# Moving work across the seam between two blocks of a hybrid attention and expert kernel: output weights' subtraction, context outputs, first latent exponentials

## The reference, cut to what matters

```
qkv = (x * (1 + scale) + shift) @ w_in          # 8 neighbourhood heads, 4 differential heads
context:  dense attention and differential attention over the 128 context keys
latent:   neighbourhood attention (window + context keys + relative bias), and
          differential attention over context and latent keys:  softmax(q1 k1) - lambda * softmax(q2 k2)
o = concat(na_o, rms_norm(df_o) * g * (1 - lambda_init)) @ w_out
x = layer_norm(alpha * x + gate * o);  then 16 experts, each choosing its tokens, SwiGLU;  layer_norm
```

## Time and profile before

| | us |
|---|---|
| median of 3 runs (lowest, highest) | 1845.98 (1843.43, 1846.46) |
| time of the profiled execution | 1844.35 |
| its span in the trace | 1842.5 |
| TensorE busy | 1782.4 (97%) |
| VectorE busy | 1119.4 (61%) |
| ScalarE busy | 589.7 (32%) |
| GpSimd busy | 101.4 (6%) |
| mean granted clock of TensorE | 0.985 |

### The profile page before, as it was taken

The page is one execution under the profiler, slowest core; times in us unless marked ns, Lnnn a source line. Parts: engine busy times, 40 slices in busy tenths (PEclk is TensorE's granted clock), DMA queues, the critical chain, the costliest instruction groups (busy, mean ns, idle before and its releaser), DMA issues.

```text
span 1842.5 us, 37553 instructions
## 1 busy us (share of the span) xinstructions
PE 1782.4 (97%) x15484; PEld 739.9 (40%) x15484; DVE 1119.4 (61%) x3401; ACT 589.7 (32%) x1265; POOL 101.4 (6%) x86
## 2 busy tenths in 40 slices
PE   8999989993999999999999999999999999999998
PEld 8999867762222222222222222222222222222222
DVE  3766856666647474746556474747474664747474
ACT  3222446551323232233223232322232222323233
POOL 0000132204000000000000000000000000000000
PEclk9999989996999999999999999999999999999999
DMA  9644331236999999999999999999999999999992
GB/s 381 251 166 166 121 122 60 64 147 263 375 407 406 411 422 407 424 410 425 410 425 405 425 405 416 415 409 425 404 425 410 425 405 425 408 422 410 415 415 105
DMA packets 102986, 637.13 MB, mean 346 GB/s; under 512 B 11584, under 2 KB 21824, under 8 KB 30112
## 3 DMA queue, kind: packets, MB, share of 16 engines
q1 hardware_dynamic: 97696, 618.19, 81.8%
q0 software_dynamic: 4832, 16.50, 3.2%
q10 hardware_dynamic: 288, 0.03, 0.0%
HBM read 620.02 MB, written 13.88 MB: 344 GB/s over the span
## 4 chain that ended last, share of the span: by engine, by line
PE 74%; ACT 1%; DVE 0%; issue 0%; DVEq 0%; ACTq 0%
PE ps L1630 49%; PE ps L1645 25%; ACT place L1736 0%; ACT place L1732 0%; ACT place L1739 0%; ACT place L1734 0%; DVE place L1747 0%; PE ps L1614 0%; DVE place L1807 0%; DVE place L1823 0%; PE ps L1674 0%; DVE place L1804 0%; DVEq L1573 0%; ACT place L1729 0%; ACT place L1711 0%
## 5 line engine op out<-in xcount | busy, mean ns | idle before, releaser
L1630 PE MATMUL ps<-place 128*32 128x512 f32 x4872 | 530.2, 594 | 0.8 <-DVE place L1747 0.8
L1760 DVE STREAM_TRANSPOSE place<-place 32x64 f32<-32x64 f32 x2112 | 496.6, 235 | 32.8
L1630 PE MATMUL ps<-ring,place 128*32 128x512 f32 x3576 | 388.9, 592 | 0.0
L1630 PEld LDWEIGHTS ps<-place 128*32 128x32 f32 x4872 | 146.4, 110 | 378.4 <-issue 377.3
L1691 ACT ACTIVATE place<-ps 64x512 f32<-64x512 f32 x176 | 104.6, 594 | 499.9 <-PE ps L1630 499.9
L1645 PE MATMUL ps<-place 128*32 128x512 f32 x2424 | 263.5, 592 | 0.0
L1630 PEld LDWEIGHTS ps<-ring,place 128*32 128x32 f32 x3576 | 107.3, 110 | 276.4 <-issue 276.4
L1752 DVE TENSOR_TENSOR place<-ps,place 96x512 f32<-96x512 f32 x176 | 120.8, 687 | 132.3 <-ACT place L1692 129.8
L1645 PE MATMUL ps<-ring,place 128*32 128x512 f32 x1800 | 196.4, 592 | 0.0
L1777 DVE TENSOR_TENSOR place<-ps,place 64x512 f32<-64x512 f32 x15 | 10.2, 683 | 285.0 <-ACT place L1711 285.0
L1645 PEld LDWEIGHTS ps<-place 128*32 128x32 f32 x2424 | 72.7, 110 | 187.4 <-issue 187.4
(11 more groups left out here) (230 smaller groups left out, 1471.8 us busy)
## 6 DMA issues: line engine op xcount, KB each, us to landing
place<-in_w_exp SPq DMA_DIRECT2D x304, 1024.0 KB, 15.1
ring<-in_w_exp SPq DMA_DIRECT2D x224, 1024.0 KB, 15.3
ring<-in_w_late SPq DMA_DIRECT2D x16, 1024.0 KB, 11.3
ring<-in_w_in SPq DMA_DIRECT2D x12, 1024.0 KB, 6.7
ring<-in_w_ada SPq DMA_DIRECT2D x7, 1024.0 KB, 10.6
ring<-in_w_out SPq DMA_DIRECT2D x4, 1024.0 KB, 6.5
place<-in_near_bias SPq DMA_DIRECT2D x16, 256.0 KB, 3.4
ring<-in_xT SPq DMA_DIRECT2D x4, 640.0 KB, 9.2
```

What stands on the lines that cost most here:

```text
L1630: mm = eng.matmul((up_side(Q) if side else up_main(Q))[quad(q)], X[:, e % 2, half * HALF_K + k, quad(g)], w[:, k * 512:(k + 1) * 512], sta ...
L1760: ins = eng.transpose(hT[quad(q), b * FPC:(b + 1) * FPC, quad(g)], hid[quad(g), Q % 2, 2 * q * QUAD:2 * (q + 1) * QUAD])
```

## The change

Five things move, and nothing is added or left out:

1. TensorE: the four `ctx_weigh` stand between the high and the low part of the value block of token tile 3, the scores of unit 4 behind that, and the value block of tile 4 whole behind the scores.
2. VectorE: both `split_out` leave the first block. They run in steps 5 and 6 of the second, behind that step's maxima and ahead of what is due there.
3. VectorE: the context outputs and the maxima of unit 4 stand ahead of the additions to the modulation.
4. ScalarE: `round_out(1)` goes ahead of the copy of value tile 3.
5. ScalarE: the four exponentials of unit 4 go from the start of the second block to the end of the first, ahead of the last value copy.

```diff
--- before.py
+++ after.py
@@ -311,6 +311,14 @@
             for m in range(2, 4):
                 eng.tensor_reduce(stat[:, u, m:m + 1], columns(m), AX_X, ALU.max, negate=True).then_inc(max_done, 1)
 
+        def probs(u, part):
+            return Pb[:, u % 2, PARTS[part][1]:PARTS[part][2]]
+
+        def exp(eng, u, part):
+            eng.wait_ge(max_done, 4 * u + (3 if part % 2 == 0 else 4))
+            eng.activation(probs(u, part), columns(part), ACT.Exp, bias=stat[:, u, part:part + 1],
+                           scale=-1.0 if part < 2 else 1.0, accum_out=total[:, u, part:part + 1]).then_inc(p_done, 1)
+
         def ctx_columns(u, m):
 
             c0 = (u % 2) * 2 * CTX + (m // 2) * CTX
@@ -524,14 +532,16 @@
                     for n, src in enumerate((kna, kdf)):
                         mm = eng.transpose(ps[:, 6, n * P:(n + 1) * P], src[:, i, 0:CTX], ident)
                     mm.then_inc(kctx_ready, 1)
-                    values(i, 3)
                     if last:
+                        values(i, 3, low=False)
                         for u in range(GROUPS):
                             ctx_weigh(eng, u)
-                    values(i, 4, low=not last)
-                eng.wait_ge(cache_landed, 48 * GROUPS)
-                scores(eng, GROUPS)
-                values(GROUPS - 1, 4, high=False)
+                        values(i, 3, high=False)
+                        eng.wait_ge(cache_landed, 48 * GROUPS)
+                        scores(eng, GROUPS)
+                    else:
+                        values(i, 3)
+                    values(i, 4)
 
             @block.scalar
             def _(eng):
@@ -615,9 +625,13 @@
                     if i >= 2:
                         eng.wait_ge(k_stored[i % 2], 16 * (i // 2))
                     eng.activation(kout[:, i % 2, :], ps[:, 6, 0:256], ACT.Copy).then_inc(kctx_copied, 1)
-                    copy_values(i, 3)
                     if i + 1 == GROUPS:
                         round_out(eng, 1)
+                        copy_values(i, 3)
+                        for part in (0, 2, 1, 3):
+                            exp(eng, GROUPS, part)
+                    else:
+                        copy_values(i, 3)
                     copy_values(i, 4)
 
             @block.vector
@@ -725,16 +739,14 @@
                         if i == GROUPS - 1 and n == 0:
                             ctx_combine(eng, 3)
                     eng.wait_ge(rope_done, 2 * i + 2)
-                split_out(eng, 0)
+                for u in range(GROUPS):
+                    outputs(eng, u, ps[:, u, :], O_even)
+                maxima(eng, GROUPS)
                 eng.wait_ge(late_used, LATE_PER * GROUPS)
                 rest = flat[:, 2 * EARLY:, :]
                 chain(eng.tensor_tensor(rest, rest, b_flat[:, 2 * EARLY:].unsqueeze(2).broadcast_to([P, 6 * KT - 2 * EARLY, 2]),
                                         ALU.add))
                 chain(eng.tensor_scalar(modT[:, 4], modT[:, 4], 1.0, None, ALU.add))
-                for u in range(GROUPS):
-                    outputs(eng, u, ps[:, u, :], O_even)
-                split_out(eng, 1)
-                maxima(eng, GROUPS)
 
         places.pop().close()
         places.append(ctx.enter_context(ExitStack()))
@@ -869,9 +881,6 @@
         def due(what, k):
 
             return WHEN[what].index(k) if k in WHEN[what] else None
-
-        def probs(u, part):
-            return Pb[:, u % 2, PARTS[part][1]:PARTS[part][2]]
 
         TURNS = ((0, 0, 3), (1, 3, 3), (2, 6, 3), (2, 9, 2))
 
@@ -1191,12 +1200,6 @@
 
             @block.scalar
             def _(eng):
-                def exp(u, part):
-                    eng.wait_ge(max_done, 4 * u + (3 if part % 2 == 0 else 4))
-                    eng.activation(probs(u, part), columns(part), ACT.Exp, bias=stat[:, u, part:part + 1],
-                                   scale=-1.0 if part < 2 else 1.0, accum_out=total[:, u, part:part + 1]
-                                   ).then_inc(p_done, 1)
-
                 def copy_p(u, n):
                     part, c0, cs = TURNS[n]
                     use = turn_no["p", u, n]
@@ -1233,19 +1236,17 @@
                     eng.wait_ge(logits_read, s + 1)
                     eng.activation(aff[:, t, :], aff[:, t, :], ACT.Exp, accum_out=asum[:, t:t + 1]).then_inc(aff_exp, 1)
 
-                for part in (0, 2, 1, 3):
-                    exp(GROUPS, part)
                 for k in range(GROUPS + 1, STEPS):
                     now = k < UNITS
                     copy_p(k - 1, 0)
                     copy_p(k - 1, 1)
                     if now:
-                        exp(k, 0)
-                        exp(k, 2)
+                        exp(eng, k, 0)
+                        exp(eng, k, 2)
                     copy_p(k - 1, 2)
                     if now:
-                        exp(k, 1)
-                        exp(k, 3)
+                        exp(eng, k, 1)
+                        exp(eng, k, 3)
                     copy_p(k - 1, 3)
                     if due("route", k) is not None:
                         raise_logits(due("route", k))
@@ -1446,6 +1447,8 @@
                             if v == 0:
                                 chain(ins)
                         ins.then_inc(fold_done, 1)
+                    if k - GROUPS - 1 in range(2):
+                        split_out(eng, k - GROUPS - 1)
                     if due("squares", k) is not None:
                         squares(due("squares", k))
                     if due("turn o", k) is not None:
```

## The result

The changed kernel takes 1849.18 us, the median of 22 runs (lowest 1846.58), where the kernel before takes 1846.41 in 22 runs beside it (1843.43 to 1849.03). One of the changed kernel's 22 runs, 2105.71 us at a mean granted clock of 0.841, was slow and is not in the ratio. The ratio is 1.0018, with a 95% interval of 1.0012 to 1.0024. That is 3.3 us slower by the ratio, with 2.2 to 4.4 as its interval; the two medians differ by 2.8. It lies within the 0.2% that the forecast called the same and within its range, but at +1.4 the forecast named only about half of it or less.

The account below looks back on a forecast made before the run. TensorE was taken to bound the kernel (74% of the span, expert matmuls). Switch +0.1, second table -0.3, ScalarE queue -1.3, half clock +0.7, meeting GpSimd +2.2 gave +1.4 us: 1846.5 from 1845.1, range 1843.0 to 1849.6.

Parts of the forecast that it names:

- (a): At the seam: switch 0.1 us later, exponentials' 2.8 us beneath value matmuls, TensorE restarts at 227.3 in place of 229.90.
- (b): Behind the switch: the bias table binds, second unit's maxima only 0.3 us sooner, its first exponential 1.5 us sooner.
- (c): Step 6's scores all at half clock: of 1.5 us about 0.8 is left, maxima end at 245.1 for 245.9.
- (e): Step 6: subtraction and scalings meet GpSimd's additions, +1.8 us, or +0.6 with only one addition ahead of the scalings.
- (d): Moved subtractions, 2.28 us of VectorE each: the one in step 5 worth nothing, the one in step 6 free alone.
- slower rival: Step 6: GpSimd's two 2.79 us multiplications also go ahead of scalings, +4.5 to +7.3 us; chance 0.12.
- small gain: Step 6: GpSimd's additions come at other moments or don't overtake VectorE, -0.3 to -1.1 us; chance 0.27.
- whole gain: At the seam: the table does not bind and all 2.6 us arrive; chance 0.05.

Follow-up runs that it names:

- e5: Changed kernel with the second subtraction behind the scaling and the bias tables of units 5 and 6 loaded and added in the first block: 1841.57 us, ratio 0.9974.
- e4: Changed kernel with GpSimd's bias additions for units 8 and 9 replaced by a fill that reads nothing: 1846.86 us, ratio 1.0004.
- e1: Changed kernel with only the second subtraction moved behind the scaling of the context heads in step 6: 1846.08 us, ratio 1.0000.
- e7: Changed kernel with GpSimd's two 1024-column multiplications two steps later: 1848.8 us, one run.
- e12: Like e5, but with the second subtraction ahead of the scaling again, as in the changed kernel: 1840.19 us, one run.
- e6: Kernel before with only the bias tables of units 5 and 6 loaded and added early, in the first block: 1848.01 us, ratio 1.0012.
- e11: Changed kernel with six unread matmuls in TensorE's step 6 wait, ahead of the turns: 1844.99 us, one run; stretch 45.37 us.
- e9: Like e5, plus unread matmuls in three TensorE waits of step 6 (two, two and one): 1838.38 us, ratio 0.9958.
- e3: Kernel before with only the two subtractions moved to steps 5 and 6: 1849.03 us, ratio 1.0015.

## Why the prediction was half right

Each step is on the clock of before; after's time is its own less 1.54.

| step of the prediction | predicted | after |
|---|---|---|
| (a) TensorE starts again | 227.3 | 227.26 |
| (b) maxima of the second unit | 232.3 | 232.35 |
| (b) its first exponential | 234.3 | 234.20 |
| (b) total-weight product | 237.8 | 237.69 |
| (c) maxima of step 6 end | 245.1 | 245.43 |
| (e) subtraction ends | 247.9 | 248.30 |
| (e) scalings end | 251.3 | 252.21 |
| (e) turns done, product starts | 253.3 | 254.03 |
| change up to there | +1.8 | +2.75 |
| longer half clock behind it | 0 to 1.3, taken as 0 | +0.60 |

**(a) and (b) were right** within 0.1 us, including the sign of what the table lets through. e5 shows that it was the table that took the gain there: with it early, the maxima follow the combine at once.

**(c) was too kind by 0.3.** The scores of step 6 ran wholly at half clock (0.50 at 242 to 244) and took back 1.1 of the 1.6 us, not 0.7.

**(d) held as far as the runs show.** The first subtraction takes 2.28 us beside nothing that waits. That the second would be free alone no run shows outright, since none has it ahead of the scaling without GpSimd beside it. In e4 the 1.7 us that are left are as much as the two collisions that are left, 0.9 and 0.8.

**(e) had the right mechanism and the wrong size**, and this is the step that failed. e1 shows the mechanism by order alone, e4 by taking two additions away. In the terms of the sum, the total-weight product ahead of step 6 came 1.57 us sooner where -1.5 stood. Half clock took back 1.08 up to step 6's maxima where +0.7 stood, and another 0.60 behind the turns where nothing stood. The meeting with GpSimd measured +3.24 (8.60 less 5.36) where +2.2 stood. That makes the 3.35. Two things in the last term were mis-sized. The first is the number of scalings held: two, I wrote, and three were. The multiplication of line 992 held the third for about 0.85 us (e7: 0.85 less without it). I had ruled this out by the combine of 251.96, which took its ordinary 0.89. But that combine started 2.36 us after the multiplication did, and the trace has others that started sooner: in e1 the 640-column combine of 251.25, 0.19 us behind a multiplication, took 1.54. One row that is not held, late in a long instruction, shows nothing of that instruction's start. And the rows of before had the sign of it, in GpSimd's second multiplication, which started within that same combine and was itself held, 3.10 us for 2.76 in after:

```profile
252.38 3.10 POOL L984 TENSOR_SCALAR place<-place 128x1024 f32<-128x1024 f32 x1
```

The second is my choice in the range. From +1.8 I went down to +1.4, since fewer collisions seemed possible, and put the longer half clock in the range but not in the sum. All that was left open fell on the same side. The +1.8 itself was counted from 251.5, the modelled end of the second turn, where the product of before started at 251.28; its own 253.3 is +2.0 on that row. The scalings then ended 0.9 us later than I wrote, by (c) and the third scaling, and the turns took 0.2 less, which makes the 2.75.

**The numbers around it.** Half of the three runs' spread of 3.0 is 1.5 and not the 1.0 that the range uses at its lower end; nothing hangs on it. The forecast stood on 1845.1 for before, where 22 runs give 1846.41, so 1.3 of the 2.7 us between 1846.5 and 1849.18 are of that base. And the time lies in the range because its upper end was drawn to the slower rival (1849.6); the forecast's own end, +3.1, was 1848.2.

**The rivals.** The small gain did not come: it would have needed subtraction and scalings to miss most of the additions, and even in e12, where they do, the order costs 1.1. Nor did the whole gain, since the table did bind. The slower rival was half right. GpSimd's multiplication does hold VectorE out, but for its first 0.85 us and not for 2.79 or 5.6, so it is part of the loss and not another case. With its full price it would have given 4.5 to 7.3 us.

The Trainium skill, under "SBUF — State Buffer", section "Who interferes with whom", has the shared pair held for an operation's whole length. For GpSimd's additions the runs agree: each scaling that met one ended with it. For the multiplication by one number per partition they don't: in e4 it took 2.79 us from 248.08, and all four scalings were over by 250.05.

**The time.** The stretch, +3.35, agrees with the ratio, +3.3. The two profiled spans differ by twice that, 1849.1 against 1842.5. Of the 6.6 us, 1.5 lie ahead of the stretch, in code that the change doesn't touch, and some 2 among the experts. There one execution had its full clock about 1 us later, which explains a part of the 2 at most. I would have told the wrong story from the two spans alone.

## What to carry to other kernels

Work that "has room" on its own engine must also be laid against what the other engine of a shared resource does at that moment: write down GpSimd's instructions for those microseconds, and put the short operations that someone waits for ahead of the long one that no one waits for. When a wait is shortened, look at what it was waiting behind, here a table whose load was issued only at the switch: moving that load and its addition was worth 3.2 us of this stretch (e5 against e1), while the seam's new order alone was worth 0.3, and the early table alone nothing that the time shows (e6). When two single profiles are compared, look first at whether the clock took the same course in both: between e5 and e12 it moved one point of the stretch by 1.2 us and hid what the order cost. And price a standstill of TensorE with what it runs at behind it; a few matmuls without a reader, short enough to end before the wait does, gave back 2.3 us in e11 and more in e9.

## What was new about the hardware

GpSimd's one-input multiplication of 1024 columns takes 2.79 us, but it holds a two-input operation of VectorE only when this meets its first part. Scalings that started with it took 0.83 (e4) and 0.84 (after) longer; a 640-column combine that came 0.19 us behind took 1.54 for 0.89 (e1), one 0.51 us behind took 1.21 (e6), and the last scaling of after, 1.10 us behind, and a combine 2.36 us behind (before) had their plain length. Each that was held was held until about 0.85 us behind the multiplication's start. Why it ends there no run shows.

Where both engines have work in a row, they take turns: addition, scaling, addition, scaling in after, each waiting for the other. Four scalings of 0.3 us between three of GpSimd's operations cost 3.79 us in after and in e11.

How long the half clock stood behind a standstill was not the same in two executions of the same code. Behind the switch TensorE started again at 229.90 in before and at 229.78 in e3, with the same instructions and no pause up to the clock's rise in either, and the clock was full from about 236.1 in before and from about 233.0 in e3. At the start of the experts half clock stood for about 3.6 us after 457.79 in before and for about 4.7 us after 462.34 in after. Both kernels, in the stretches behind that start (before first, then after):

```profile
461.00:463.00 2.00, 2.00 (x20) 0.56 (x16) 0.00 (x0) 0.00 (x0) 0.00 (x0) 0.90 0.04 8
463.00:465.00 2.00, 2.00 (x24) 0.60 (x20) 0.00 (x0) 0.02 (x1) 0.00 (x0) 1.00 0.59 205
```
```profile
463.00:465.00 2.00, 2.00 (x16) 0.49 (x12) 0.00 (x0) 0.38 (x2) 0.00 (x0) 0.50 0.50 145
465.00:467.00 2.00, 2.00 (x16) 0.49 (x12) 0.00 (x0) 0.00 (x0) 0.00 (x0) 0.50 0.03 8
```
